# The first norm's weight vector as one row that TensorE spreads, and fewer warm-up matmuls, in a one-core decoder layer

## The reference

```python
def rmsnorm(x, g):
    y = x * lax.rsqrt(jnp.mean(x * x, axis=-1, keepdims=True) + EPS)
    return y * g

h = x
proj = rmsnorm(h, norm_mix_g) @ w_in
y_a = gmlp_chunk_mixer(proj[..., :2048], gm_v_norm_g, gm_ws, gm_bs, gm_out_norm_g)
y_b = ssd_mixer(proj[..., 2048:], conv and SSD parameters, ssd_norm_g)
h = h + concatenate([y_a, y_b]) @ w_out
hid = relu(rmsnorm(h, norm_mlp_g) @ w_ff1)
h = h + (hid * hid) @ w_ff2
h = h + sigmoid(rmsnorm(h, ple_norm_g) @ w_ple_gate) * (p @ w_ple_proj)
return rmsnorm(h, final_norm_g)
```

## Time and profile before

| | |
|---|---|
| median of three runs | 757.28 us (757.15 to 757.96) |
| the profiled execution, its own time | 759.14 us |
| its span, first to last instruction | 757.4 us |
| TensorE busy | 739.5 us, 98% of the span |
| VectorE, ScalarE, GpSimd busy | 62%, 50%, 16% |
| moved by DMA | 107.14 MB, mean 141 GB/s |

### The profile page before, as it was taken

How to read it: one execution, slowest core, us unless ns; L and a number is a source line. 1 busy time by engine, 2 the same in 40 slices (tenths; PEclk the granted TensorE clock), 3 DMA queues, 4 the chain that set the end, 5 groups by cost and what they waited for, 6 DMA issues and landing times. The chain is left out here.

```text
span 757.4 us, 8676 instructions
## 1 busy us (share of the span) xinstructions
PE 739.5 (98%) x3396; PEld 608.2 (80%) x3396; DVE 470.4 (62%) x504; ACT 378.4 (50%) x508; POOL 117.7 (16%) x92
## 2 busy tenths in 40 slices
PE   8999999999999999999999999999999999998896
PEld 7888877878877888888888888888788888886784
DVE  5556885566668576546454952586256744498854
ACT  5534456644665733314565524562257326554565
POOL 1021310766455000000012000200002000100000
PEclk9999999999999999999999999999999999999999
DMA  9732223442242263101968693477727691883211
GB/s 335 186 96 85 83 84 115 131 145 85 99 151 62 78 217 117 57 29 39 378 194 166 164 278 114 112 166 250 195 55 157 194 261 55 168 232 129 84 56 55
DMA packets 48256, 107.14 MB, mean 141 GB/s; under 512 B 4692, under 2 KB 6360, under 8 KB 48216
## 3 DMA queue, kind: packets, MB, share of 16 engines
q1 hardware_dynamic: 41352, 85.59, 33.9%
q0 software_dynamic: 5632, 16.78, 12.3%
q10 hardware_dynamic: 1232, 4.23, 1.6%
HBM read 89.77 MB, written 4.23 MB: 124 GB/s over the span
## 5 line engine op out<-in xcount | busy, mean ns | idle before, releaser
L985 DVE TENSOR_TENSOR w_lo<-w_raw,w_hi 128x1024 fp32r<-128x1024 f32 (+1 forms) x64 | 87.5, 1375 | 32.3 <-ACT w_hi L596 31.6
L1471 PE MATMUL acc<-w_hi,a_hi 128*128 128x512 f32 x256 | 104.3, 408 | 0.0
L1473 PE MATMUL acc<-w_hi,a_lo 128*128 128x512 f32 x256 | 100.1, 391 | 0.0
L1471 PE MATMUL acc<-b_hi,ring_hi 128*128 128x512 f32 x256 | 99.7, 390 | 0.4 <-DVE h L1332 0.4
L1472 PE MATMUL acc<-w_lo,a_hi 128*128 128x512 f32 x256 | 99.8, 390 | 0.0
L1472 PE MATMUL acc<-b_lo,ring_hi 128*128 128x512 f32 x256 | 99.6, 389 | 0.0
L1473 PE MATMUL acc<-b_hi,ring_lo 128*128 128x512 f32 x256 | 99.6, 389 | 0.0
L1276 DVE TENSOR_TENSOR ring_lo<-ring_raw,ring_hi 128x1024 fp32r<-128x1024 f32 x32 | 39.0, 1225 | 73.2 <-ACT ring_hi L663 73.0
L663 ACT ACTIVATE ring_hi<-quarter 128x1024 fp32r<-128x1024 f32 x56 | 56.5, 1050 | 51.3 <-PE acc L1473 31.3
L596 ACT ACTIVATE w_hi<-w_raw 128x1024 fp32r<-128x1024 f32 (+1 forms) x64 | 64.6, 1025 | 33.6 <-PE acc L1473 31.3
L1276 DVE TENSOR_TENSOR ring_lo<-quarter,ring_hi 128x1024 fp32r<-128x1024 f32 x56 | 65.9, 1220 | 17.0 <-ACT ring_hi L663 17.0
(11 more groups left out here) (227 smaller groups left out, 1435.3 us busy)
## 6 DMA issues: line engine op xcount, KB each, us to landing
quarter<-in_w_ff SPq DMA_DIRECT2D x40, 512.0 KB, 4.9
w_raw<-in_w_in SPq DMA_DIRECT2D x36, 512.0 KB, 3.9
ring_raw<-in_w_ff SPq DMA_DIRECT2D x32, 512.0 KB, 5.8
quarter<-quarter POOLq DMA_DIRECT2D x24, 512.0 KB, 6.2
w_raw<-in_w_out SPq DMA_DIRECT2D x16, 512.0 KB, 3.4
h<-in_x SPq DMA_DIRECT2D x8, 512.0 KB, 4.4
seg<-cs_dram ACTq DMA_DIRECT2D x8, 512.0 KB, 4.0
quarter<-in_w_ff POOLq DMA_DIRECT2D x8, 512.0 KB, 7.0
```

The lines of the kernel that those rows point to most:

```text
L985: dve.tensor_tensor(w_lo[:, half, 2 * p:2 * p + n, :], w_raw[:, p, 0:n, :], w_hi[:, half, 2 * p:2 * p + n, :].bitcast(F32), ALU.subtract). ...
L1471: pe.matmul(dst, st[0], mv[0], start=start, stop=False)
L1473: return pe.matmul(dst, st[1], mv[0], start=False, stop=stop)
```

## The change

The first thing that SyncE issues is now a copy of `norm_mix_g` as one row of 4 KB into partition 0 of `gain` slot 1; its broadcast into slot 0 is gone. TensorE runs 4 warm-up matmuls, waits for the row, multiplies a row of 128 ones by it in two f32 matmuls of 512 columns (into `acc` banks 2 and 3, every partition then holds the vector), runs 2 more warm-ups, the transposes, and 4 warm-ups in place of 10. VectorE copies the two banks into `gain` slot 0 ahead of the first norm. The `v` norm's gain, which overwrites slot 1, is issued behind a wait for the two matmuls. The counts of the later waits on `gain_landed` are shifted to match.

```diff
-WARM = 10
...
+        gain_spread, gain_copied = sem("gain_spread"), sem("gain_copied")
...
+            sp.dma_start(gain[0:1, 1, :], a["norm_mix_g"]).then_inc(gain_landed[1], 16)
             load_x(0)
-            load_gain(a["norm_mix_g"][0], 0)
             for p in range(3):
                 first_piece(p)
...
+            sp.wait_ge(gain_spread, 2)
             load_gain(a["gm_v_norm_g"][0], 1)
...
-                    pool.wait_ge(gain_landed[1], 16)
+                    pool.wait_ge(gain_landed[1], 32)
...
-                slot, use = ((0, 1), (0, 3), (1, 3))[n]
+                slot, use = ((0, 0), (0, 2), (1, 4))[n]
                 c = s if n < 2 else TILES[s]
-                if s == 0:
+                if n and s == 0:
                     dve.wait_ge(gain_landed[slot], 16 * use)
...
             dve.memset(eps[:], EPS).then_inc(eps_ready, 1)
+            dve.wait_ge(gain_spread, 2)
+            dve.tensor_copy(gain[:, 0, :], acc[:, 2:4, :].rearrange("p a n -> p (a n)")).then_inc(gain_copied, 1)
+            dve.wait_ge(gain_copied, 1)
 
             normed(0, 0)
...
-            for i in range(WARM):
+            for i in range(4):
+                pe.matmul(acc[:, i % 2, 0:P], ident[:], ones[:], start=True, stop=True)
+            pe.wait_ge(gain_landed[1], 16)
+            for i in range(2):
+                pe.matmul(acc[:, 2 + i, :], ones[0:1, :], gain[0:1, 1, 512 * i:512 * i + 512], start=True, stop=True
+                          ).then_inc(gain_spread, 1)
+            for i in range(2):
                 pe.matmul(acc[:, i % 2, 0:P], ident[:], ones[:], start=True, stop=True)
             turn_norm(0, 0)
-            for i in range(WARM):
+            for i in range(4):
                 pe.matmul(acc[:, i % 2, 0:P], ident[:], ones[:], start=True, stop=True)
+            pe.wait_ge(gain_copied, 1)
```

More of the change, by code:

```diff
@@ L1170, in _ @@
                     dve.wait_ge(m_rstd_ready, 1)
-                    dve.wait_ge(gain_landed[0], 32)
+                    dve.wait_ge(gain_landed[0], 16)
                     for i in range(NS):
@@ L1235, in yb_scale @@
                 dve.wait_ge(m_rstd_ready, 2 + g)
-                dve.wait_ge(gain_landed[1], 32)
+                dve.wait_ge(gain_landed[1], 48)
                 for i in range(NS):
@@ L1446, in _ @@
                 if i == 0:
-                    dve.wait_ge(gain_landed[0], 16 * 4)
+                    dve.wait_ge(gain_landed[0], 16 * 3)
                 dve.tensor_tensor(y[:, s, at], h[:, s, at], gain[:, 0, at], ALU.mult).then_inc(h_gain, 1)
```

## The result

The changed kernel takes **759.85 us** in the median of nine runs (759.25 to 762.24), against 757.28 for the kernel before in the runs beside them (756.8 to 758.37): 1.0033 of it, with a 95% interval from 1.0021 to 1.0045. It is 2.6 us slower. The forecast was 757.7, the range ended at 759.7, and "slower" had a chance of 0.16. The prediction was wrong.

What follows compares the result with a forecast made beforehand. TensorE, 98% busy, was taken as the bound, with the start deciding: norm +2.2 us, 0.9 given back, late lo halves, so piece 3's products +0.4. Added to the 757.28 median: 757.7 us, range 756.3 to 759.7.

Steps and rivals of the forecast that it cites:

- the place to look at is the first group: At the start, the change counts only by how much earlier or later the first group of products gets through.
- The row lands at 2.6 us: At the start, the 4 KB gain row, issued at 0.81, lands at 2.6 us; 5.0 was kept for a rival.
- Row products of 0.86 us a pass at 1.2 GHz, copy of 1.22: Ahead of the first norm, four one-row passes take 3.4 us, VectorE's copy 1.22; first tile normed at 9.95.
- Transposes that start at 10.0 at 2.4 GHz: The first tile's eight transposes start at 10.0 us at the high clock, so ScalarE's evacuations finish at 11.75.
- rival (a): Slower: clock still 1.2 GHz when the first transposes start at 10.0; +1.2 to +2.4 us, middle 758.9; chance 0.27.
- a low clock past 12: Early in the kernel, TensorE's clock being low past 12 us was named as one sign of a wrong prediction.
- The 0.9 us that I gave back on ScalarE: At the first evacuations, faster transposes return 0.9 of the norm's +2.2 us, leaving +1.3 on ScalarE's queue.
- That run stands 1.86 over the median, so I forecast 757.28 + 0.4: For the whole kernel, +0.4 us, summed on the profiled run, was added to the median: 757.7 us.
- The broadcast's end is worth nothing by itself: At the first norm, dropping the 512 KB broadcast ends a 0.59 us wait, but the gain's longer way hides it.
- the cut of warm-ups: Around the first transposes, 20 fewer warm-up passes are worth nothing, because the lo halves are late next, not TensorE.
- The waits at SyncE's queue and the renumbered counts cost nothing: At SyncE, the v-norm gain and second weight batch have time to spare; changed waits only renumber counts; no cost.
- Where rule and trace part: On TensorE's clock: trace has transposes counting as busy, against the skill; both let a 2.1 us hole cost nothing.

Runs made afterwards that it cites:

- e12: The kernel before with 7 warm-up matmuls in the second half of the late 3.5 us hole; 756.75 us (0.9989).
- e13: The changed kernel with 7 warm-up matmuls in the second half of the late 3.5 us hole; 758.59 us (1.0013).
- e6a: The kernel before, unchanged, profiled once more; 759.67 us in that profile.
- e6b: The kernel before, unchanged, in another additional profile; 756.95 us in that profile.
- e10: The changed kernel without warm-ups ahead of the row products, each half copied when its bank is full, then 5 warm-ups; 758.60 us (1.0007).
- e1: The kernel before with the changed kernel's mix of passes ahead of the transposes, one-row products on constants nobody waits for; 759.47 us (1.0014).
- e2: The kernel before with the same mix of passes as e1, but 128 rows in the 512-column products; 757.54 us (0.9997).
- e9: The changed kernel, unchanged, run and profiled again; 759.72 us (1.0030).
- e4: The kernel before with the first norm's gain broadcast replaced by ones that VectorE writes; 756.99 us (0.9994).
- e5: The kernel before with 4 warm-up matmuls in place of 10 behind the first transposes; 757.43 us (0.9999).
- e11: The changed kernel with 10 warm-up matmuls in place of 4 behind the first transposes; 761.77 us (1.0048).
- e3: The changed kernel with 6 warm-up matmuls in place of 2 between the spreading products and the transposes; 760.55 us (1.0022).
- e7: The changed kernel with 128 rows in the spreading products, 127 of them zeros, and the row issued later, behind the zeroing; 760.79 us (1.0037).
- e14: The kernel before with 14 warm-up matmuls ahead of the first transposes, 4 behind, and the late hole filled; 756.02 us (0.9976).

## Why the prediction was wrong

- **That the place to look at is the first group: right.** e12 against e13 leaves 2.0 us when the late hole is filled in both. That the waits further on take up no delay holds too, but 0.4 us of the 3.9 for `h` in the earlier trace rows, at 538 us, is one that e6a and e6b do not have.
- **The row lands at 2.6 us: near.** In e10 nothing else kept TensorE, and it waited until 2.33.
- **Row products of 0.86 us a pass at 1.2 GHz, copy of 1.22: right.** Four took 3.7 us in all, and the norm ended at 10.29, 0.3 over the forecast.
- **"Transposes that start at 10.0 at 2.4 GHz": the step that failed.** It was put down without a row for it. The argument against rival (a) was that TensorE would work without a hole for 6.1 us, longer than the 3.0 ahead of the rise at 10.85; but most of those 6.1 us are one-row passes, and e1 against e2 shows that such passes left the clock at 1.2 GHz, where passes of 128 rows let it rise. The transposes took 1.97 us, the clock rose at 14.24, and the prediction's own sign of being wrong, a low clock past 12, was there. The 0.9 us that I gave back on ScalarE did not come: evacuations to 12.95, not 11.75; lo half 3 at 18.86, not 17.7; piece 3 at 18.94, not 17.75. That is 1.2 of the miss of 2.15. In e9 and e13 the clock stayed low further into the products, 0.75 more. This is rival (a) within its price of +1.2 to +2.4 on the first profile (+1.6 and +2.3 on piece 3); it had 0.27 and should have been the forecast. Its "middle: 758.9" does not follow from that price: the middle is +1.8, 759.1.
- **"That run stands 1.86 over the median, so I forecast 757.28 + 0.4": the second step.** The distance was taken for a constant. The time of an unprofiled execution is about 1.7 us over its span too; the profiled run of before was itself a long one, over all nine timed runs beside the result. Its start (17.36) is near the late end of what before does, 16.17 to 17.54 in five profiles of kernels with its front (three of the five rose early), and it had a fall at the late hole and the 0.7 us of waits ahead of it. These waits hid part of the loss in the profiled pair, which stands only 0.76 apart (759.14 and 759.90). The changed kernel's start was at 18.9 or 19.7 in all three of its profiles. So each rival priced against 17.36 was priced too kindly, by up to 1.2 us for a run with an early rise, and the range ended 0.15 us short. How much of the miss is due to this is not shown, as the early clock of timed runs is not recorded.
- **The broadcast's end is worth nothing by itself: right** in sign (0.57 us on the norm in e4, spent by the longer way), **and the cut of warm-ups "worth nothing": right behind an early rise** (e5, 16.25 against 16.17), and probably wrong at 1.2 GHz, where e11 is 1.4 us over e9 with overlapping intervals. Piece 0 came at least 1.8 us sooner, not 1.3, and that brought nothing.
- **The waits at SyncE's queue and the renumbered counts cost nothing: nothing in the profile speaks against it.** The conv rows are read 1.6 us later than before, because the groups ahead of them are, and TensorE does not wait for them. No run takes these waits apart.
- **Where rule and trace part.** On transposes the runs lean to the trace: in before and e6b the clock rose behind a hole, 1.8 us of transposes and 1.3 or 1.8 us of warm-ups, where 2.9 us of warm-ups in e3, and 4.6 in before, had not raised it. What the prediction read out of the rule that it quotes on them, 1.2 GHz into the products, did come, but e1 against e2 puts it down to the one-row passes. On the hole the measurement parts from the rule: holes of 2.03 us (e6a) and 2.39 us (e7) cost the clock, and one of 3.5 us did not in e6b. The Trainium skill ("TensorE: Matmul & The Clock Gate", "Why this matters for your kernels") warns of gaps over about 3 us. On the length of a product with few rows they agree: four passes took 3.78 us with one row and 3.49 with 128. The same table of the Trainium skill says that a product with 32 rows takes the time of one with 128.

What stays open: why the early rise was kept in e5 and e12 over holes of 1.84 and 1.50 us and lost in e6a over one of 2.03; how often each happens in before's timed runs, whose early clock is not recorded; and whether a few rows more than one would have raised the clock, as only one and 128 were tried.

## What to carry to other kernels

Work that is put on TensorE to save a transfer has to be priced at the clock that it will find, and products of one row did not serve as warm-up here: where passes are to raise the clock, give them all 128 rows. Before summing against one profile, take a second and a third of the same kernel; where the granted clock differs between them, the typical run and not the profiled one is the base. The only clear gain (e14, 1.6 us) came from filling both holes; the late one alone brought about 1.0 us, at the edge of what twelve runs can tell, and the early one alone nothing measurable.

## What the runs showed of the hardware

- Four f32 passes of 1 x 512 kept TensorE busy for 3.7 us and the clock did not rise with them: it rose at 11.08 us at the earliest in seven profiles (13.04 in e1, 14.24 and 15.87 in the changed kernel). With 128 rows in their place it rose at 6.82 (e2), and at 8.15 even where 127 of the rows were zeros (e7).
- The clock's fall at one and the same hole of 3.5 us lasted 0, 3.4 or 6.8 us in different executions of one program, and the stretch from there to the last product took 45.2, 46.8 and 47.9 us with it. With its second half filled (1.8 us left idle) there was no fall in the three profiles taken (some timed runs may have had one); of the fourteen unfilled, three had none.
- A row of 4 KB, issued first, had landed 1.5 us after its issue at 0.81 (e10); behind a tile and with traffic, issued at 2.03, it took until 5.1 (e7).
